# Fused two-block kernel: rows of the moving tiles lengthened by 16, 8, 32 and 4 bytes

## The reference, cut to what matters

```
h = x + merged(rmsnorm(x) @ w_in) @ w_o          # gated linear attention, convolution, windowed attention
h = h + (silu(gate) * val) @ w_down              # gate, val: conv of rmsnorm(h) @ w_up
h = [16 meta tokens, rmsnorm(h)]                 # second block, 528 columns
h = h + [hgrn2, mamba2](rmsnorm(h) @ w_in_2) @ w_out_2
h = h + (silu(gate) * val) @ ffn_w_down_2
out = rmsnorm(h)[:, 16:]
```

## Time and profile before

| | us |
|---|---|
| median of three runs | 1768.79 |
| the profiled execution's own time | 1769.76 |
| its span, first to last instruction | 1767.9 |
| TensorE matmul busy | 1739.9 |
| VectorE busy | 1172.4 |
| ScalarE busy | 717.3 |

### The profile page before, as it was taken

One profiled execution on the slowest core, in us unless ns is written; L12 is line 12 of the kernel. 1 busy time (PEld: TensorE's weight loads), 2 busy tenths in 40 slices (PEclk: granted clock), 3 DMA queues, 4 the chain that ended last, 5 costly groups with the idle time before them and its releaser, 6 DMA issues.

```text
span 1767.9 us, 27352 instructions
## 1 busy us (share of the span) xinstructions
PE 1739.9 (98%) x11022; PEld 1530.2 (87%) x11022; DVE 1172.4 (66%) x1809; ACT 717.3 (41%) x1101; POOL 11.8 (1%) x12
## 2 busy tenths in 40 slices
PE   9999999999999999999999999999998999999997
PEld 7877887788888888888899999999998999999885
DVE  6666656566568777734577767788797877777332
ACT  6433433332353333333545454544454433333221
POOL 0000000000000000000000000000000000000000
PEclk9999999999999999999999999999999999999999
DMA  6222232223333333333222222222122233333331
GB/s 203 82 73 78 77 88 91 84 73 97 95 96 96 98 100 99 97 96 99 78 74 73 69 73 63 62 75 80 60 73 68 76 96 96 96 92 89 108 95 60
DMA packets 44716, 153.81 MB, mean 87 GB/s; under 512 B 6032, under 2 KB 6416, under 8 KB 44592
## 3 DMA queue, kind: packets, MB, share of 16 engines
q1 hardware_dynamic: 44592, 152.08, 28.4%
HBM read 149.96 MB, written 2.10 MB: 86 GB/s over the span
## 4 chain that ended last, share of the span: by engine, by line
PE 80%; DVE 11%; ACT 4%; DVEq 2%; issue 1%; ACTq 1%; DMA 0%; SPq 0%; POOL 0%
PE ps L678 79%; DVE arena L1421 3%; ACT arena L1031 2%; DVE w_lo L1418 2%; DVEq L1970 1%; DVE arena L1428 1%; PE ps L682 1%; ACTq L1401 1%; ACT w_hi L1031 1%; DVE arena L1418 1%; DVE h_res L1418 1%; DVE u_lo L1638 0%; ACT L1036 0%; DVE arena L1435 0%; DVE r_bc L1418 0%
## 5 line engine op out<-in xcount | busy, mean ns | idle before, releaser
L678 PE MATMUL ps<-u_hi,w_hi 128*128 128x258 f32 (+3 forms) x2376 | 639.7, 323 | 1.4 <-DVE arena L1421 1.2
L678 PE MATMUL ps<-u_lo,w_hi 128*128 128x258 f32 (+3 forms) x2376 | 631.0, 319 | 0.4 <-DVE u_lo L1638 0.3
L678 PE MATMUL ps<-u_hi,w_lo 128*128 128x258 f32 (+3 forms) x2368 | 631.3, 320 | 0.0
L1418 DVE TENSOR_TENSOR w_lo<-w_raw,w_hi 128x1024 fp32r<-128x1024 f32 (+1 forms) x280 | 341.4, 1219 | 150.4 <-ACT w_hi L1031 139.0
L678 PEld LDWEIGHTS ps<-u_hi,w_hi 128*128 128x128 f32 (+1 forms) x2376 | 392.2, 188 | 41.2 <-issue 5.1
L678 PEld LDWEIGHTS ps<-u_lo,w_hi 128*128 128x128 f32 (+1 forms) x2376 | 393.9, 188 | 33.9 <-DVE u_lo L1638 1.3
L678 PEld LDWEIGHTS ps<-u_hi,w_lo 128*128 128x128 f32 (+1 forms) x2368 | 391.2, 188 | 31.2 <-issue 0.2
L1031 ACT ACTIVATE w_hi<-w_raw 128x1024 fp32r<-128x1024 f32 (+1 forms) x281 | 294.1, 1047 | 297.5 <-PE ps L678 290.3
L1428 DVE SCALAR_TENSOR_TENSOR ffn<-full,par,ffn 128x512 f32<-128x512 f32 (+2 forms) x176 | 132.2, 751 | 80.9 <-ACT ffn L1031 77.7
L1031 ACT ACTIVATE arena<-arena 128x528 f32<-128x528 f32 (+11 forms) x189 | 96.2, 531 | 217.3 <-DVE arena L1421 86.4
L1031 ACT ACTIVATE ffn<-full,par 128x512 f32<-128x512 f32 x88 | 67.7, 769 | 268.7 <-DVE full L1421 268.7
(11 more groups left out here) (160 smaller groups left out, 1509.4 us busy)
## 6 DMA issues: line engine op xcount, KB each, us to landing
w_raw<-weights SPq DMA_DIRECT2D x278, 512.0 KB, 3.5
h_res<-xT SPq DMA_DIRECT2D x8, 256.0 KB, 5.4
outT<-h_res SPq DMA_DIRECT2D x6, 256.0 KB, 2.4
cst<-consts SPq DMA_DIRECT2D x1, 730.0 KB, 8.8
w_raw<-weights SPq DMA_DIRECT2D x2, 256.0 KB, 4.1
outT<-ffn SPq DMA_DIRECT2D x2, 256.0 KB, 2.6
seg<-consts SPq DMA_DIRECT2D x1, 256.0 KB, 8.6
par<-params SPq DMA_DIRECT2D x1, 240.0 KB, 6.9
```

The source lines that it names most:

```text
L678: return nc.tensor.matmul(out, lhsT, rhs, start=start, stop=stop)
L1418: return V.tensor_tensor(out, a, b, op)
```

## The change

Rows get longer, and with them the tiles; what is computed and the order of all instructions stay.

```diff
-U_WIDE = 9 * LINE
+U_WIDE = 9 * LINE + 4
...
-        y_hi = sb("y_hi", [P, 12, SEQ], F32R, s1)
-        y_lo = sb("y_lo", [P, 12, SEQ], F32R, s1)
+        y_hi = sb("y_hi", [P, 12, SEQ + 8], F32R, s1)[:, :, 0:SEQ]
+        y_lo = sb("y_lo", [P, 12, SEQ + 8], F32R, s1)[:, :, 0:SEQ]
...
-        m_hi = sb("m_hi", [P, KD, SEQ], F32R, s1)
-        m_lo = sb("m_lo", [P, KD, SEQ], F32R, s1)
+        m_hi = sb("m_hi", [P, KD, SEQ + 1], F32R, s1)[:, :, 0:SEQ]
+        m_lo = sb("m_lo", [P, KD, SEQ + 1], F32R, s1)[:, :, 0:SEQ]
...
-        a_hi = sb("a_hi", [P, FT, SEQ], F32R, s2)
-        a_lo = sb("a_lo", [P, FT, SEQ], F32R, s2)
+        a_hi = sb("a_hi", [P, FT, SEQ + 2], F32R, s2)[:, :, 0:SEQ]
+        a_lo = sb("a_lo", [P, FT, SEQ + 2], F32R, s2)[:, :, 0:SEQ]
...
-        v_hi = sb("v_hi", [P, KD, U_WIDE], F32R, s3)[:, :, V_FIRST:]
-        v_lo = sb("v_lo", [P, KD, U_WIDE], F32R, s3)[:, :, V_FIRST:]
+        v_hi = sb("v_hi", [P, KD, U_WIDE], F32R, s3)[:, :, V_FIRST:V_FIRST + T2 - USED]
+        v_lo = sb("v_lo", [P, KD, U_WIDE], F32R, s3)[:, :, V_FIRST:V_FIRST + T2 - USED]
```

## The result

The changed kernel takes 1787.04 us (median of 4 runs, 1785.5 to 1788.49) where the kernel before took 1767.93 on the same chip: a ratio of 1.0106, 95% interval 1.0092 to 1.0121. It is slower by 19 us. The forecast was 1763.0, with 1745 to 1776 as its range, and "slower" had a chance of 0.20. In what follows a distance in bytes is that of a moving row's start from the weights' start, modulo 256; a distance in ns is the time from one matmul's start to the next one's.

A forecast was written before the change was run, and what follows sets the result against it. The prediction took TensorE's matmul count times start-to-start distance to bound the kernel. Its only nonzero term, -6.0 us on the 512-column matmuls, against the profiled 1769.76, which stands 1.0 above the median, gave 1763 us, range 1745 to 1776.

The forecast's parts named there:

- What bounds the kernel: Whole kernel: time is the number of TensorE matmuls times their start-to-start distance, 226.6 ns for 512 columns; waits are small.
- the price of the 512-column matmuls: Matmuls of u, a, y and m: rows at changing distances were to make 3,984 matmuls cheaper, -6.0 us in all.
- an excess of 11.8 in place of 13.3: Excess in ns per 512-column matmul: 13.3 before, 11.8 (mean of the mixed case) expected after the change.
- the large gain: Rival on the 512-column matmuls: their whole excess gone, -53.0 us; chance 0.10.
- The bounds of that step: 512-column matmuls: -13.1 us at the even halves' 10.0, -53.0 with the whole excess gone; above, the slower rival.
- the bounds of the halves: Matmuls of 264, 258 and 256 columns: +3.1 us if the 264s go to 11.8, -6.6 if the others reach 10.0.
- the 231.7 ns after an interruption: 512-column matmuls following small ones, 148.52 to 149.91 us: six distances of 231.7 ns each before 226.6 returns.
- the far half of that rival: Slower rival with all 512-column matmuls having to settle, +20 us, 1789 us; 0.10 left out of the range.
- The rival that ends slower: 512-column streams lose their steady state at rows starting elsewhere, 5.1 ns each; 1776 us for one in three; chance 0.21.
- Distances don't matter: Rival for all matmul streams: every term is 0, 1768.8 us by the median; chance 0.33.
- The halves: 1,728 matmuls of 264 columns and 3,648 of 258 and 256: already at mixed distances, so 0 us.
- Writers, ffn, stores: ScalarE and VectorE writes of longer rows cost 0, staying hidden; shifted ffn and its end stores 0, within 0.2 us.

The follow-up runs named there:

- e1: Kernel before with rows at constant distances ahead of the weights, without steps: u and v 128 bytes, a 8, y 32, m 4; 1794.59 us, ratio 1.0154.
- h1: Kernel before with all rows of u, v, a, y and m moved to 4 bytes ahead of the weights; 1816.33 us.
- g1: Kernel before with only the split weights moved 252 bytes further, so every row is 4 bytes ahead of them; 1794.15 us.
- f3: Kernel before with rows at constant distances from the weights: u and v 32 bytes, a 96, y 16, m 252; 1783.26 us.
- f4: Kernel before with every tile, the weights too, moved 96 bytes further, distances between them kept at 0; 1767.3 us, ratio 0.9991.
- g3: Kernel before with the second feed-forward's u columns shifted, so its halves lie at 24 and 32 bytes; median 1769.12 us, ratio 1.0005.
- h3: The unchanged kernel of g3 executed once more to profile another execution; that execution took 1770.24 us.
- f2: Kernel before with rows at constant distances from the weights: u and v 192 bytes, a 240, y 64, m 248; 1790.85 us.

## Why the prediction was wrong

- **What bounds the kernel** held: none of TensorE's largest waits moved by more than 1.5 us, the writers cost 752 and 693 ns and ffn's stores took 2.6 us to land as before, and the time is the matmuls' distance from start to start.
- **The step that failed is the price of the 512-column matmuls.** I put them 1.5 ns lower, at an excess of 11.8 in place of 13.3, -6.0 us. In u, a and m they went from 226.5 to 226.9 ns up to 232.0 to 232.7, +5.1 to +6.2 ns each, in y by 2.8, about +21 us in all. No run shows the 13.3, the 11.8 and the 10.0 ns, nor the time per column that they are counted from. What the runs show is 226.6 ns for 512 columns, 118.9 for the halves at 248 and 0 bytes and 120.0 for those at 0 and 32, and no 512-column matmul of the dense streams of before started less than 224 ns after the one ahead of it. Such an excess compares across column counts, 512 against 258 and 264, and no row of before had a 512 at another distance; so no row said that 226.6 was the unfavourable case. The map has eight distances that are dearer than 0 by 6 ns or more, two dearer by 2 to 5, and one equal; none is cheaper, so the large gain, with its 0.10, didn't come either.
- **The bounds of that step** were both on the side of a gain, and like the bounds of the halves they are made of the same excess; the lowest distance that any layout gave the 512s, 226.5 ns, is that of before. The row that pointed the other way was in the prediction, the 231.7 ns after an interruption: a stream that isn't in the steady state of distance 0 paid 5.1 ns more, and the changed kernel pays about that all the time. That both have one cause is likely, not shown. As the only row of before with dense 512s out of step it should have set the upper bound of the range; the far half of that rival, 1789 us for all of them, is within 2 us of the result and was left out at 1776. That agreement is in part luck, as e1 and h1 stand 8 and 29 us above the changed kernel.
- **The rival that ends slower** named the right size, and the wrong reason in part. It is not the step from row to row that costs (e1 has no such step and is slower yet, 1794.59 us), but the distance to the weights. The 3.4 ns between h1 and g1, both at 4 bytes, are not explained by it.
- **Distances don't matter** is refuted by g1, f3 and f4 together: move the weights alone (g1, a at 233.3 ns) or the rows alone (f3, a at 233.3) and the stages change, move all (f4, a at 226.5) and none does. At the dearest distance the price is 10 ns in 227 (h1).
- **The halves** held as a sum, near 0: -0.3 ns for most, +1.3 for the 264s, about +1 us.
- **Writers, ffn, stores**: 0, as said; 693 and 752 ns as before.
- The range missed by 11 us, because the sum took a gain of 1.5 ns where a loss of 5 to 6 stood, and the upper bound was worked out from one settling matmul in three.

What stays open is the cause. Two measurements say that a place alone doesn't fix the price of a matmul. Rows that lie alike modulo 256 bytes don't cost alike: e1's u rows alternate between 229 and 237 ns, and in the kernel before, all at 0, the matmuls after an interruption are 224 to 236 ns apart until they settle at 226 and 227. And one layout took two values, 116.7 and 119.9 ns (g3, h3). A model would have to give 226.7 at 0 and 252, 229.0 at 64, 231.4 at 16 and 233.2 to 236.7 at the other eight, and none was found that does. Distances other than the twelve of the map weren't tried. Nor was a stream without weight loads beside it: g1 shows that the place of the stored weights counts, and no run shows that it counts through their load.

## What to carry to other kernels

Here TensorE is dense with fp32r matmuls of 512 columns, each with its own weight load, and the start of the moving row against the start of the weights modulo 256 bytes was worth up to 4% of the distance between them (236.7 against 226.7 ns), and equal starts were, with 252 bytes, the best of twelve tried; in a kernel like this one it is the first thing to keep when a tile is padded or inserted. Price an unknown layout from the same instruction form: in f3 the 258-column halves got cheaper (118.9 to 116.7 ns) and the 512s dearer (226.9 to 233.2). And when a stream has a steady state, take what it costs out of step, which an interruption shows (231.7 ns here), as one end of the range; the dearest layouts, at 236.7, went beyond even that.

## What the runs showed of the hardware that wasn't expected

The steady distances of the constant layouts tried cluster at 226.7, 229.0, 231.4, 233.3 and 236.7 ns; h1 holds 236.7 in u and a alike, and f3's, e1's and f2's different distances give the same 233.2. One layout showed two steady distances in two executions of the same program (116.7 and 119.9 ns for halves, g3 and h3), so the single profile of g3, at 1763.07 us, showed a gain that its median, 1769.12, doesn't have. And 4 bytes ahead of the weights (236.7 ns) is, with 240, the dearest place of those tried, and 4 behind (226.7 ns) is, with 0, the cheapest.
